# One layer of a hybrid trunk: w_up of three feed-forward groups by Strassen's algorithm, in pairs of column blocks

## What is computed

```python
hn = rms_norm(x, p['norm_mlp_pre'])
u = jnp.square(jax.nn.relu(hn @ p['w_up'])) @ p['w_down']   # w_up 1024 x 4096, w_down 4096 x 1024
x = x + rms_norm(u, p['norm_mlp_post'])
```

## Time and profile before

| | before |
|---|---|
| median of 3 runs | 1524.05 us (1521.7 to 1524.39) |
| time of the profiled execution | 1522.61 us |
| its span, first to last instruction | 1520.9 us |
| mean granted TensorE clock | 0.999 of full |
| up phase of groups 1, 2 and 3 | 56.31 us each |
| down phase | 54.4 us each |

### The profile page before, as it was taken

One profiled execution on the slowest core, in us unless ns is written; L12 is line 12 of the kernel. 1 busy time (PEld: TensorE's weight loads), 2 busy tenths in 40 slices (PEclk: granted clock), 3 DMA queues, 4 the chain that ended last, 5 costly groups with the idle time before them and its releaser, 6 DMA issues.

```text
span 1520.9 us, 25469 instructions
## 1 busy us (share of the span) xinstructions
PE 1490.4 (98%) x9798; PEld 1392.1 (92%) x9798; DVE 691.1 (45%) x1190; ACT 604.9 (40%) x1100; POOL 10.8 (1%) x25
## 2 busy tenths in 40 slices
PE   6999999999999999999999999999999999999998
PEld 6988999989999899999999999998998998998986
DVE  5555555542358774334454553346423323323335
ACT  5333333322147773224654641235541441531532
POOL 1000000000000000000000000000100000000000
PEclk9999999999999999999999999999999999999999
DMA  5556445432222322232332322343122222222222
GB/s 161 152 135 164 126 126 152 114 81 76 73 59 68 87 59 84 69 103 69 116 101 69 114 86 82 91 165 92 42 83 70 81 71 84 69 83 70 80 88 82
DMA packets 225089, 143.61 MB, mean 94 GB/s; under 512 B 7718, under 2 KB 211239, under 8 KB 225020
## 3 DMA queue, kind: packets, MB, share of 16 engines
q1 hardware_dynamic: 225028, 142.75, 32.6%
HBM read 129.90 MB, written 12.84 MB: 94 GB/s over the span
## 4 chain that ended last, share of the span: by engine, by line
PE 84%; DVE 5%; ACT 4%; issue 3%; DMA 2%; SPq 1%; DVEq 0%; ACTq 0%
PE psum L598 55%; PE psum L1010 18%; DMA w_raw<-in_w_in_dram 2%; PE psum L783 1%; PE psum L755 1%; PE psum L646 1%; PE psum L939 1%; DVE arena L1941 1%; ACT arena L1395 1%; PE psum L609 1%; ACT w_hi L1197 1%; PE psum L766 1%; PE psum L977 1%; PE psum L715 1%; PE psum L726 1%
## 5 line engine op out<-in xcount | busy, mean ns | idle before, releaser
L598 PE MATMUL psum<-XH,w_hi 128*128 128x320 f32 x1872 | 588.4, 314 | 3.8 <-ACT arena L1385 1.8
L598 PE MATMUL psum<-XH,w_lo 128*128 128x320 f32 x1872 | 578.4, 309 | 0.0
L598 PE MATMUL psum<-XL,w_hi 128*128 128x320 f32 x1872 | 578.3, 309 | 0.0
L1665 DVE TENSOR_TENSOR w_lo<-w_raw,w_hi 128x1024 fp32r<-128x1024 f32 x177 | 216.5, 1223 | 354.5 <-ACT w_hi L1197 353.8
L598 PEld LDWEIGHTS psum<-XH,w_hi 128*128 128x128 f32 x1872 | 351.5, 188 | 17.0 <-issue 8.9
L598 PEld LDWEIGHTS psum<-XL,w_hi 128*128 128x128 f32 x1872 | 351.7, 188 | 0.8
L598 PEld LDWEIGHTS psum<-XH,w_lo 128*128 128x128 f32 x1872 | 351.4, 188 | 0.0
L1197 ACT CAST w_hi<-w_raw 128x1024 fp32r<-128x1024 f32 x177 | 185.2, 1047 | 308.5 <-PE psum L1010 154.1
L1010 PE MATMUL psum<-w_hi,YL 128*128 128x512 f32 x280 | 109.0, 389 | 0.0
L1010 PE MATMUL psum<-w_hi,YH 128*128 128x512 f32 x280 | 109.0, 389 | 0.0
L1010 PE MATMUL psum<-w_lo,YH 128*128 128x512 f32 x280 | 108.9, 389 | 0.0
(11 more groups left out here) (274 smaller groups left out, 1703.0 us busy)
## 6 DMA issues: line engine op xcount, KB each, us to landing
w_raw<-in_w_in_dram SPq DMA_DIRECT2D x88, 512.0 KB, 3.8
w_raw<-in_w_up_dram SPq DMA_DIRECT2D x32, 512.0 KB, 4.1
w_raw<-in_w_down_dram SPq DMA_DIRECT2D x32, 512.0 KB, 3.5
w_raw<-in_w_branch_dram SPq DMA_DIRECT2D x24, 512.0 KB, 3.8
arena<-in_cache_fox_k_dram SPq DMA_DIRECT2D x8, 1024.0 KB, 6.2
arena<-in_cache_fox_v_dram SPq DMA_DIRECT2D x8, 1024.0 KB, 7.9
out_dram<-arena SPq DMA_DIRECT2D x16, 256.0 KB, 2.4
arena<-in_state_gla_dram SPq DMA_DIRECT2D x4, 1024.0 KB, 5.4
```

The lines of the kernel that those rows point to most:

```text
L598: mm = pe.matmul(Z[h][:, 0:HT], w[s][:, k, :], x[:, k, h * HT:(h + 1) * HT], start=(k == 0 and i == 0), stop=(k == KT - 1 and i == 2))
L1665: dve.tensor_tensor(dst, src, h.bitcast(F32), ALU.subtract).then_inc(w_lo, 1)
```

## The change

For groups 1, 2 and 3 the up phase takes its 8 column blocks in 4 pairs. A pair is a product of a 2 x 2 block matrix of weights (two column blocks x two halves of the model dimension) with a 2 x 2 block matrix of activations (two halves of the model dimension x two halves of the tokens), and Strassen's algorithm (in Winograd's form) makes it with 7 products in place of 8. A product is 4 tiles x 3 matmuls of 128 x 320, 12 matmuls. Around the products stand:

- four sums of weights for each pair (`S1` to `S4`, 128 x 512 each), on GpSimd from the two raw blocks of the pair (`weight_sums`), each in new raw buffers `PRAW` in the space of `X2`. `X2` is therefore stored to DRAM behind group 0's w_up loads (`spill`), and loaded again in the last group's down phase, behind its fourth w_down load.
- four sums of activations (`T1` to `T3`, `T4`), made once in group 0: ten sums on VectorE, 128 x 1280 each, two after each of the blocks 0 to 4; then four high parts on ScalarE and four low parts on VectorE during group 0's down phase.
- high and low parts of 3.5 weight blocks for each pair (A11|A12, S2|S1, S3|S4, and the half block A22), where 2 blocks were split before (`pair_hi`, `pair_lo`).
- one copy of product 1 on ScalarE and seven sums on VectorE for each pair, each of one product in PSUM and one tile in SBUF (`pair_sum`), after which the four quarters of output get relu, square, high and low parts as before (`pair_u`), relu now from SBUF.

The order in a pair is given by code on each engine. The third unit's low part (`pair_lo(p, l, 2)`) stands ahead of the first sums of outputs.

```diff
+            def pair(g, l):
+                ...
+                pe.wait_ge(pw_lo, (p * 4 + 1).v)
+                product(g, l, 1, A11, B11)
+                product(g, l, 2, A12, B21)
+                pe.wait_ge(pw_lo, (p * 4 + 2).v)
+                product(g, l, 3, S2, T2)
+                product(g, l, 4, S1, T1)
+                pe.wait_ge(pw_lo, (p * 4 + 4).v)
+                product(g, l, 5, S3, T3)
+                product(g, l, 6, S4, B22)
+                product(g, l, 7, A22, T4P)
...
+                up(0, g)
+                plus(s1, h12, h11, ALU.subtract)
+                plus(t1, l12, l11, ALU.subtract)
+                lo(b + 2, b.c % 2)
+                up(1, g + 1)
...
+            def weight_sums(q, l):
+
+                p = q + l
+                pool.wait_ge(pw_in[l % 2], ((p + -l).half() * 32 + (32 * (l // 2) + 32)).v)
+                m0, m1 = PRAW[l % 2]
+                a11, a12, a21, a22 = m0[:, 0:KH, :], m0[:, KH:KT, :], m1[:, 0:KH, :], m1[:, KH:KT, :]
+                if l > 0 or p.terms or p.c > 0:
+                    pool.wait_ge(pw_lo, (p * 4 + -2).v)
+                pool.tensor_tensor(S1, a21, a22, ALU.add).then_inc(s_step, 1)
+                pool.wait_ge(s_step, (p * 2 + 1).v)
+                pool.tensor_tensor(S2, S1, a11, ALU.subtract).then_inc(s_sum, 1)
+                if l > 0 or p.terms or p.c > 0:
+                    pool.wait_ge(pw_lo, (p * 4).v)
+                pool.tensor_tensor(S3, a11, a21, ALU.subtract).then_inc(s_step, 1)
+                pool.wait_ge(s_step, (p * 2 + 2).v)
+                pool.wait_ge(s_sum, (p * 2 + 1).v)
+                pool.tensor_tensor(S4, a12, S2, ALU.subtract).then_inc(s_sum, 1)
...
+                    if l > 0:
+                        pair_u(p + -1, l - 1, 3)
+                    pair_lo(p, l, 2)
+                    dve.wait_ge(p1_kept, (p + 1).v)
+                    pair_sum(p, l, 3, KU2, KP1, P6)
+                    pair_sum(p, l, 3, c11, KP1, P2)
+                    if l > 0:
+                        pair_u(p + -1, l - 1, 2)
+                    dve.wait_ge(c_sum, (p * 7 + 1).v)
+                    pair_sum(p, l, 5, KU3, KU2, P7)
+                    dve.wait_ge(c_sum, (p * 7 + 3).v)
+                    pair_sum(p, l, 5, c22, KU3, P5)
+                    pair_sum(p, l, 5, c12, KU2, P5)
+                    pair_u(p, l, 0)
+                    if l < 3:
+                        pair_lo(p + 1, l + 1, 0)
+                    else:
+                        lo(b, b.c % 2)
+                    dve.wait_ge(c_sum, (p * 7 + 5).v)
+                    pair_sum(p, l, 6, c12, c12, P3)
+                    pair_sum(p, l, 7, c21, KU3, P4)
+                    if l < 3:
+                        pair_lo(p + 1, l + 1, 1)
+                    else:
+                        lo(b + 1, (b.c + 1) % 2)
+                    pair_u(p, l, 1)
+                    if l < 3:
+                        pair_lo(p + 1, l + 1, 3)
```

More of the change, by code:

```diff
@@ L362, in build @@
         ORD = (0, 1, 4, 2, 3)
+        U_PLACE = ((0, 0), (1, 1), (1, 0), (0, 1))
+        BANK_READ = (2, 2, 1, 5, 3, 6, 7)
         @blk.sync
@@ L569, in _, with pair_load @@
-            up_loads(Lin(B_MLP), 0, KT // 2)
[L570 to L573, removed]
+                n, c = i // NKC, i % NKC
+                s = (B_MLP + i) % 2
+                load(b + i, s, w[:, c * KC_W:(c + 1) * KC_W, n * HD:(n + 1) * HD], wide(raw[s][:, :, :]))
+            def pair_load(q, l, g):
+                p = q + l
+                if p.terms or p.c >= 2:
+                    sp.wait_ge(pw_lo, (p * 4 + -4).v)
+                for m in range(2):
+                    c0 = (2 * l + m) * P
+                    cols = slice(g * D + c0, g * D + c0 + P) if isinstance(g, int) else bass.ds(g * D + c0, P)
+                    sp.dma_start(PRAW[l % 2][m][:, :, :], w_up_v[:, :, cols]).then_inc(pw_in[l % 2], 16)
@@ L1080, in rows_free @@
+            def rows_free(g, t):
+                some = bool(g.terms) or g.c > 0
+                if some and t == 0:
+                    pe.wait_ge(c_sum, (g * 28).v)
+                if not some and t in (1, 2):
+                    pe.wait_ge(z_free[t - 1], B_OUT + KT)
                 if t >= 3:
                     pe.wait_ge(dn_free, (g * (2 * NT) + (t - 2)).v)
-            def group(g, last=False):
[L1085 to L1093, removed]
+            B11, B21 = ([v[:, j * KH:(j + 1) * KH, 0:HT] for v in (XH, XL)] for j in range(2))
@@ new lines, in _, with product @@
+            T4P, B22 = ([v[:, j * KH:(j + 1) * KH, HT:T] for v in (XH, XL)] for j in range(2))
+            T1, T2, T3 = ([v[:, :, :] for v in t] for t in T_PART)
+            def product(g, l, n, w, x):
+                p = (g + -1) * 4 + l
+                i = 7 * l + n
+                if i in (1, 4, 7):
+                    pe.wait_ge(dn_free, (g * (2 * NT) + {1: -5, 4: -2, 7: 0}[i]).v)
+                if i > 8:
+                    pe.wait_ge(c_sum, (p * 7 + (BANK_READ[(n - 9) % 7] - 7 * (1 + (n == 1)))).v)
+                for k in range(KH):
+                    for j, (wi, xi) in enumerate(((0, 0), (0, 1), (1, 0))):
+                        mm = pe.matmul(prod_bank(l, n)[:, 0:HT], w[wi][:, k, :], x[xi][:, k, :],
+                                       start=(k == 0 and j == 0), stop=(k == KH - 1 and j == 2))
+                mm.then_inc(prod, 1)
@@ L1094, in group @@
+            def group(g, last=False):
+                for l in range(4):
+                    pair(g, l)
                 down(g, last)
@@ L1594, in up, with group_zero @@
                     act.copy(YH[:, bass.ds(j, 1), half], UQ[:, half].unsqueeze(1)).then_inc(u_hi, 1)
[L1596 to L1603, removed]
+            def group_zero():
+                b, z, g = Lin(B_MLP), Lin(B_OUT), Lin(0)
+                up(z, 0, g, FIRST_UP)
                 with step.loop(KT // 2 - 1, 4) as i:
@@ L1615, in group @@
+            def group(g, last=False):
+                b = g * KT + (B_MLP + KT)
+                pairs(g)
                 for i in range(2, NKC if last else N_ROW):
                     rows_done(g, i - 2)
-                    hi_wide(b + (KT + i), (b.c + i) % 2)
+                    hi_wide(b + i, (b.c + i) % 2)
                 if last:
```

273 lines of the change are left out of this document (231 added, 42 removed).

## The result

The changed kernel takes 1503.01 us, the median of four runs (1502.88 to 1505.36), against 1522.96 us for the kernel before, the median of four (1521.7 to 1524.39). The ratio is 0.9872, with a 95% interval of 0.9855 to 0.9889: faster by 1.3%. The profiled execution took 1503.07 us, with a span of 1501.3. One run of the kernel before, beside the first experiments, took 5099.74 us; it is left out of every ratio.

A forecast was written before the change was run, and what follows sets the result against it. TensorE's matmuls were taken as the bound in the feed-forward part. 1520.9 - 21.1 + 2.5 + 1.8 = 1504.1 us of span, 1505.8 as execution time, 1507.3 with 1.4 to the median; range 1503.5 to 1516.

The forecast's parts named there:

- the sign: Whole kernel: the change makes it faster than 1521 us, chance 0.90.
- The exclusion: Pairs: VectorE instructions with two SBUF inputs and GpSimd's sums exclude each other; TensorE waits 1.8 us, bounds 0 and 6.6.
- the step from the profiled execution to the median: Whole kernel: the median of the runs lies 1.4 us above the profiled execution, added to reach 1507.3.
- Matmuls: Up phases of groups 1 to 3: 48 fewer matmuls a group at 146.6 ns, 21.1 us less for three.
- Group 0's sums: Group 0: two sums ahead of block 2's low part lengthen TensorE's stall by 2.5 us, between 2.0 and 3.5.
- the third unit's low part ends at 7.1 instead of 6.0: Crowded pairs, two a group: under exclusion this low part comes 0.3 us too late for product 5; 6 x 0.3 = 1.8 us.
- GpSimd's sums: Sums of weights on GpSimd: 1.2 us each, upper bound 1.6; 4.8 us a pair, hidden if alone.
- The line behind product 5: Pairs: VectorE's work behind product 5 ends at 12.15 us, due at 12.17; just in time, charged 0.
- The first rival: Pairs: VectorE is late more often and TensorE waits in all 12, 2.4 to 11 us; 1509.5 to 1518, chance 0.28.
- Transfers: X2's store and load and the pairs' loads: covered, charged 0, with 0 to 2 us as bounds for X2's load.
- Nothing: Pairs: a wait of 1.4 us a pair or more eats 17 us, giving 1521 to 1527; chance 0.05.
- GpSimd is the bound: Pairs: GpSimd's sums fill a pair from 3.1 us each, slower overall beyond 3.6, 1539 us at 4; chance 0.05.

The follow-up runs named there:

- the first experiments: Follow-up runs of the changed kernel and its variants, timed beside the kernel before; the text doesn't say which of them count as first.
- e1: Changed kernel with group 0's ten sums of activations behind the low part of the next block's weights, not ahead of it: 1500.78 us, ratio 0.9861.
- e2: Changed kernel with GpSimd filling S1 to S4 with a constant in place of the four sums of weights: 1502.62 us, ratio 0.9873.
- e7: Changed kernel with GpSimd making each of a pair's four sums of weights twice: 1525.44 us, ratio 1.0038.
- e5: Changed kernel with extra VectorE sums behind product 5 in each pair, in two runs: one more sum 1509.31 us, two more 1515.23 us.
- e5_one_more: Changed kernel with one more VectorE sum of 128 x 320 behind product 5 in each pair: 1509.31 us, ratio 0.9914.
- e3: Changed kernel with the third unit's low part behind the two sums of product 3 on VectorE in each pair: 1513.71 us, ratio 0.9941.
- e5_two_more: Changed kernel with two more VectorE sums of 128 x 320 behind product 5 in each pair: 1515.23 us, ratio 0.9954.
- e4: Kernel before with ten unused sums of activations added on VectorE in group 0, ahead of the weights' low parts, without Strassen's algorithm: 1525.48 us, ratio 1.0025.
- after_again: The changed kernel once more, unaltered, beside the kernel before: 1504.27 us, ratio 0.988.

## Where the prediction failed, and where it was right

The mechanism and the sign were right, the time was not: 1503.01 lies below the range. Two steps failed. The exclusion of VectorE and GpSimd was charged with 1.8 us of waits of TensorE and caused none. And the step from the profiled execution to the median added 1.4 us that did not recur. The remaining 1.0 us came in the unchanged part and belongs to no term.

**Matmuls, -21.1 us: right.** Three phases went from 56.31 to 49.28 us, 21.1 together. Their matmuls keep the pitch of 146.6 ns, the three other engines keep up, and no phase waits.

**Group 0's sums, +2.5 us: right, and the stall has a second part.** The wait was to be 2.9 us and is 2.96; blocks 3 to 6 don't wait, as worked out with 0.24 us of room (from block 4 on the low part ends 6.5 us into the block before, where the working had 6.68). e1 takes the 2.43 us back. Not in the forecast was the lowered clock behind such a wait, 1.4 to 1.5 us in some executions. The step's working saw TensorE idle and asked only how long.

**The exclusion, +1.8 us: the term that was mis-sized. It measures 0.** The mechanism is as the prediction and the Trainium skill had it (SBUF — State Buffer, section "Who interferes with whom"): e2 and the timelines agree instruction by instruction, down to sums with an input in PSUM staying at 482 ns, and e7 shows a load of GpSimd at which low parts lengthened in this way come too late. What failed is the walk to "the third unit's low part ends at 7.1 instead of 6.0". It had VectorE through its three instructions at 5.9 us of the pair; they end at 5.3. S1 started 1.85 us into the pair beside the low part of u, not behind it at 2.3. An instruction that had waited ended 0.36 to 0.55 us behind the one that held it up, where I had added whole durations. And S2 started 0.07 us after S1's end, while VectorE's half low part was still running, not behind it. The sums themselves were longer than the 1.2 us of the walk, 1.37 and 1.62. So the low part came at 6.4 and not at 7.1, 0.5 us later than in e2, and the 0.8 us of room that the prediction itself gives took it. That is the wait that was charged and never came. The prediction was right about which pairs would be crowded, two in each group. It passed over the group's first pair because VectorE has less to do there; the exclusion holds the third unit up by 0.7 us in that pair, and leaves only 0.14.

**GpSimd's sums, 1.2 us: 1.30 alone, 1.36 to 1.55 on the mean beside VectorE.** The upper bound of 1.6 held for the means, though its working isn't given: by the earlier trace rows an input adds 0.34 us, and two make the 1.2 of the forecast. The estimate from the Trainium skill (GPSIMD Engine Reference, section "Elementwise — side-by-side cycle accounting"), 1.1 to 1.2, is 0.1 to 0.2 us low for 512 elements.

**The line behind product 5, "just in time", 0: right.** The room was 0.02 by the working, 0.26 by e5. The 0.1 us that I had put down for register work isn't to be seen between those rows. The first rival (1509.5 to 1518, chance 0.28) is near what e5_one_more, e3 and e5_two_more measured, 1509.3, 1513.7 and 1515.2, though the change itself stays short of it.

**Transfers, 0: right.** Between 1130 and 1460 us TensorE has no wait for a load, and the last down phase, in which X2 comes back, lasts 54.46 us where it lasted 54.44. The order of X2's store and load was not tried by itself.

**From the span to the median, +1.4 us: wrong as a term.** The profiled execution of before lay 1.4 us under the median of its runs, and I carried that over as if it were fixed. The profiled one of after lies 0.06 us above its median. The 1.4 was one draw from a spread of some 2.5 us. In the unchanged part ahead of the feed-forward part the two profiles differ by 1.0 us as well. Profiles of the changed kernel and its variants start those 24 matmuls anywhere from 1074.50 to 1076.98, and the two programs without the change, before and e4, both at 1077.03; so it stays open whether the 1.0 us is spread alone, though the 18.1 us of after_again speak for it. Sum of the misses in the profiled execution: 1505.8 forecast, less 1.8, less 1.0, is 1503.0, measured 1503.07. For the medians another 1.5 comes off, the 1.4 above the profiled execution that were forecast and the 0.06 by which the median lies below it: 1507.3 less 1.8, less 1.0, less 1.5 is 1503.0. With the exclusion at 0 alone the forecast would have been 1505.5, inside the range. The range's lower end, 1503.5, is the sum with the terms' lower bounds (2.0 for the stall, 0 for the exclusion) and without the 1.4. It left no more room than that for spread, and the time fell 0.5 us below. How far below is chance: after_again's median, 1504.27, lies inside.

**The other rivals.** "Nothing" needed 1.4 us of wait a pair, and there is none. "GpSimd is the bound" needed sums of 3.1 us each; at 1.4 they take 5.6 of 12.32 us. But e7 is slower than before with eight sums at some 1.7 us, a load of 13.6 us a pair, where I had put that point at 14.4 (four sums at 3.6): VectorE's lengthened low parts come on top of GpSimd's own time.

## What to carry to other kernels

When work moves to an engine that others wait for, put it behind the instruction that is awaited next, not ahead of it: ten sums cost 2.5 to 4 us on one side of a low part and nothing on the other. Removed matmuls pay in full only while every other engine keeps its dates, and it is worth knowing how near the edge is: here one more 0.5 us sum in each pair takes 4 us back. When a stretch of several engines is walked through, start each instruction where its own inputs let it start and let it fill idle time, and widen the end of the range by the spread of executions instead of adding one execution's offset. Look also for the pair that seems to have the least to do: here it is the one with 0.14 us left.

## What the runs showed of the hardware

A wait of TensorE can cost more than its length, in some executions. Eight of the profiles have the wait of 2.8 us in group 0. In two of them (the first of the change and e7) TensorE went on at full clock, with 42.50 and 42.49 us for the 288 matmuls. In four (after_again, e2, e4, e5_two_more) it went on at 1.2 GHz for some 3.3 us, and they took 43.87 to 44.04. In two (e3, e5_one_more) the fall came one gap earlier, where the 24 matmuls took 5.33 us instead of 3.80, and the 288 then took 42.50. In e1_sums_behind, where TensorE's idle time there is 2.5 us shorter, the profile shows no fall. The falls of e3 and e5_one_more stand ahead of the long wait, behind shorter gaps that the kernel before has too, so a fall isn't tied to this wait alone; what decides in which execution it comes is not shown. The Trainium skill (TensorE: Matmul & The Clock Gate, section "Part 1: The HAM clock gate") has the two levels of 1.2 and 2.4 GHz and says that what sets the clock isn't in step with the kernel, and these profiles agree with that.

Two engines that exclude each other both lose, and not equally. In the changed kernel GpSimd's sums grew from 1.30 to at most 1.55 us on the mean, while VectorE's half low part went from 0.69 to 1.24 on the mean, and to 1.79 where it met a sum. With the sums doubled GpSimd's reach 1.88 on the mean. A matmul that follows a wait is recorded for 0.41 us instead of 0.31 and pushes the next by 0.1 us, so twelve short waits cost 1.2 us beyond their own length.
